# Mixture-of-experts stage of a fused two-block kernel: tokens and results as rounded parts

## The reference, cut to what matters

```python
h = modulate(rmsnorm(x, norm2_g), shift, scale)      # 256 tokens x 1024
probs = softmax(h @ router_w)                        # 16 experts in 4 groups of 4
# best group of each token, then its two best experts; combine = their normalised weights
for e in range(16):
    he = (silu(h @ w_gate[e]) * (h @ w_up[e])) @ w_down[e]   # 1024 -> 512 -> 1024
    out = out + combine[:, e:e + 1] * he
return rmsnorm(x + gate * out, final_norm_g)
```

## Time and profile before

| | us |
|---|---|
| median of 3 runs (lowest, highest) | 1445.51 (1444.1, 1450.73) |
| the profiled execution | 1446.31 |
| its span in the profile | 1444.9 |
| TensorE busy | 1341.1 (93%) |
| VectorE busy | 1044.2 (72%) |
| ScalarE busy | 711.7 (49%) |

### The profile page before, as it was taken

One profiled execution on the slowest core, in us unless ns is written; L12 is line 12 of the kernel. 1 busy time (PEld: TensorE's weight loads), 2 busy tenths in 40 slices (PEclk: granted clock), 3 DMA queues, 4 the chain that ended last, 5 costly groups with the idle time before them and its releaser, 6 DMA issues.

```text
span 1444.9 us, 20106 instructions
## 1 busy us (share of the span) xinstructions
PE 1341.1 (93%) x7872; PEld 1182.8 (82%) x7872; DVE 1044.2 (72%) x1502; ACT 711.7 (49%) x955; POOL 0.4 (0%) x5
## 2 busy tenths in 40 slices
PE   6979799999999997899997899999699999999996
PEld 6778699999777785899996688998687888887884
DVE  5676677786787787777876747866456869687685
ACT  3432455553575656454443643433146757566563
POOL 0000000000000000000000000000000000000000
PEclk9969899999999998999998999999699999999999
DMA  8729786865587775767563442220065978878772
GB/s 329 265 81 342 210 327 242 306 248 208 204 284 256 267 261 184 264 211 259 198 216 101 130 157 94 94 88 12 28 219 174 377 248 304 280 252 331 238 268 105
DMA packets 84349, 312.89 MB, mean 217 GB/s; under 512 B 9504, under 2 KB 9728, under 8 KB 83520
## 3 DMA queue, kind: packets, MB, share of 16 engines
q1 hardware_dynamic: 82080, 298.88, 58.6%
q10 hardware_dynamic: 2176, 12.74, 2.7%
HBM read 310.54 MB, written 1.05 MB: 216 GB/s over the span
## 4 chain that ended last, share of the span: by engine, by line
PE 82%; DVE 10%; ACT 3%; DMA 3%; issue 2%; SPq 0%; DVEq 0%; ACTq 0%
PE ps L445 81%; DVE w_low L404 2%; DMA ring<-stream 2%; DVE junk L404 1%; ACT w_high L404 1%; DVE rs L404 1%; DVE t_one L404 1%; PE ps L1042 1%; DMA ring<-moe 1%; DVE y_experts L404 1%; DVE sc L404 0%; DVE sm L404 0%; DVE rout L404 0%; ACT L404 0%; DVE t_two L404 0%
## 5 line engine op out<-in xcount | busy, mean ns | idle before, releaser
L404 DVE TENSOR_TENSOR w_low<-ring,w_high 128x1024 fp32r<-128x1024 f32 x368 | 442.0, 1222 | 166.7 <-ACT w_high L404 162.3
L404 ACT ACTIVATE w_high<-ring 128x1024 fp32r<-128x1024 f32 x368 | 385.6, 1058 | 294.1 <-PE ps L445 202.3
L445 PE MATMUL ps<-x_high,w_high 128*128 128x256 f32 (+1 forms) x784 | 235.5, 300 | 27.3 <-DVE x_low L404 21.1
L445 PE MATMUL ps<-x_low,w_high 128*128 128x256 f32 (+1 forms) x784 | 232.9, 297 | 0.0
L445 PE MATMUL ps<-x_high,w_low 128*128 128x256 f32 (+1 forms) x784 | 232.7, 297 | 0.0
L404 DVE CUSTOM_DVE_ANT_0 junk<-ring,cond 128x1024 f32<-128x1024 f32 x137 | 167.1, 1222 | 33.7 <-DMA ring<-stream 25.3
L445 PEld LDWEIGHTS ps<-x_high,w_high 128*128 128x128 f32 x784 | 154.5, 197 | 36.3 <-issue 12.9
L445 PEld LDWEIGHTS ps<-x_high,w_low 128*128 128x128 f32 x784 | 154.3, 197 | 2.8
L445 PEld LDWEIGHTS ps<-x_low,w_high 128*128 128x128 f32 x784 | 154.5, 197 | 2.5
L445 PE MATMUL ps<-h_high,w_high 128*128 128x256 f32 x512 | 145.4, 284 | 1.7 <-DVE h_low L404 1.0
L445 PE MATMUL ps<-h_low,w_high 128*128 128x256 f32 x512 | 144.9, 283 | 0.0
(11 more groups left out here) (302 smaller groups left out, 1999.1 us busy)
## 6 DMA issues: line engine op xcount, KB each, us to landing
ring<-stream SPq DMA_DIRECT2D x376, 512.0 KB, 4.7
ring<-moe SPq DMA_DIRECT2D x192, 512.0 KB, 4.8
tab_two<-tab ACTq DMA_DIRECT2D x1, 2824.0 KB, 14.4
gw<-gw ACTq DMA_DIRECT2D x1, 2304.0 KB, 15.5
cond<-cvec ACTq DMA_DIRECT2D x2, 512.0 KB, 5.3
x<-xT ACTq DMA_DIRECT2D x1, 1024.0 KB, 11.6
ctx_first<-ctxT ACTq DMA_DIRECT2D x1, 1024.0 KB, 5.6
ctx<-ctxT ACTq DMA_DIRECT2D x1, 1024.0 KB, 5.0
```

Source lines behind the costliest of these rows:

```text
L404: return op(*a, **k).then_inc(self.sem, 1)
L445: return pe.matmul(out, stationary, moving, start=start, stop=stop, skip_group_check=True)
```

## The change

- **Entry.** The norm, its gain and the modulation scale become one VectorE operation for each k-tile (into `t_one`); ScalarE adds the shift, writes `t_two` and signals each pair of tiles by `x_high`; the logits start per pair, k outermost.
- **Tokens as parts.** `pe.transpose` becomes a float32 product with the identity, which leaves the PSUM banks open (no stop). ScalarE writes the high part of the tokens, TensorE subtracts it from the bank by a product with the negative identity, ScalarE writes the rest as the low part. `onehot` and `scat` become float32r. The gather makes high and low parts in banks of their own: ScalarE copies one, VectorE the other, neither waiting for the other.
- **Order.** The gather's low copies go between VectorE's two picks of an expert; `diag`'s product moves into gate(0) after its first piece, the combine weights after gate(0).
- **Results as parts.** ScalarE writes high parts of results, VectorE the low parts; `scatter` makes two products for one of float32. `result_lows` and `summed` are new calls in the loop.
- **End.** The final norm is one pass.

```diff
-        self.XT = view("x_tokens", aB + 5120, 2048).rearrange("p (b d) -> p b d", b=2)
-        self.ONEHOT = view("onehot", ...)
-        self.SCAT = view("scat", ...)
+        self.XT = tuple(rounded("x_tokens_" + n, a, 2048)... for n, a in (("high", aB + 5120), ("low", aT1)))
+        self.ONEHOT = rounded("onehot", ...)
+        self.SCAT = rounded("scat", ...)
+        self.YES = tuple(rounded("y_experts_" + n, a, 2048)... for n, a in (("high", aT2), ("low", aB + 5120)))
+        self.YS = tuple(rounded("y_single_" + n, a, 1024) for n, a in (("high", aT1 + 1024), ("low", aT1)))
...
TensorE
-    pe.wait_ge(s.t2, 4 * MOD_MOE + 4)
-    for b in range(2):
-        for k in range(KT):
+    for k in range(KT):
+        if k % 2 == 0:
+            pe.wait_ge(s.x_high, x_splits(MOD_MOE) + k // 2 + 1)
+        for b in range(2):
             ins = mm(PS[:, 4 + b, 0:NE], m.T2[:, k, b * P:(b + 1) * P], m.par("rw", k * NE, NE), k == 0, k == KT - 1)
-            ins = pe.transpose(PS[...], m.T2[:, k, b * P:(b + 1) * P], m.ident)
+            ins = mm(PS[...], m.T2[:, k, b * P:(b + 1) * P], m.ident, k % 4 == 0, False)
...
+    for b in range(2):
+        pe.wait_ge(s.xt, b + 1)
+        for c in range(2):
+            ins = mm(PS[:, 2 * b + c, :], m.NEG, m.XT[0][:, b, c * 512:(c + 1) * 512], False, True)
+        ins.then_inc(s.xt_mm, 1)
+    pe.wait_ge(s.xt, 4)
     pe.wait_ge(s.onehot, 2)
+    for r in range(4):
+        if r == 3:
+            pe.wait_ge(s.xg_high, 1)
+            pe.wait_ge(s.xg_low, 1)
+        for part in range(2):
+            for j in range(2):
+                ins = tokens(PS[:, XG_BANKS[r][part], j * 256:(j + 1) * 256], part, 2 * r + j, slice(0, 256))
+            ins.then_inc(s.xg_mm, 1)
...
     def other_tokens():
+        pe.wait_ge(s.scat, 5)
+        pe.wait_ge(s.cw, 1)
         for k in range(KT):
-            pe.wait_ge(s.xg_low, 4 if k < 4 else k + 1)
-            for b in range(2):
-                ins = mm(PS[:, 4 + k % 4, ...], m.XT[:, b, ...], m.ONEHOT[:, b, 256:CAP], b == 0, b == 1)
-            ins.then_inc(s.xg_mm, 1)
+            pe.wait_ge(s.xg_high, 4 + max(k - 1, 0))
+            tokens(PS[:, 4 + k % 2, 0:CAP - 256], 0, k, slice(256, CAP)).then_inc(s.xg_mm, 1)
+            pe.wait_ge(s.xg_low, 4 + max(k - 1, 0))
+            tokens(PS[:, 6 + k % 2, 0:CAP - 256], 1, k, slice(256, CAP)).then_inc(s.xg_mm, 1)
...
     def scatter(i, r):
+        pe.wait_ge(s.y_add, Y_LOW[i] - (i > 0 and r < 2))
...
             if i == 0:
-                mm(out, m.YE[:, 0, blk], m.SCAT[:, 0, :], True, False)
-                ins = mm(out, m.YE[:, 1, blk], m.SCAT[:, 1, :], False, True)
+                for n in range(4):
+                    ins = mm(out, m.YES[n % 2][:, n // 2, blk], m.SCAT[:, n // 2, :], n == 0, n == 3)
             else:
-                ins = mm(out, m.YS[:, blk], m.SCAT[:, i + 1, :], True, True)
+                for n in range(2):
+                    ins = mm(out, m.YS[n][:, blk], m.SCAT[:, i + 1, :], n == 0, n == 1)
ScalarE
+    for k in range(KT):
+        if k % 2 == 0:
+            act.wait_ge(s.t2, 4 * MOD_MOE + k // 2 + 1)
+        A(m.T2[:, k, :], m.T1[:, k, :], ACT.Identity, s.x_high if k % 2 else None, bias=m.MOD[:, 120 + k:121 + k], apart=True)
+    A(m.NEG, m.ident, ACT.Copy, None, scale=-1.0)
...
+    def summed(p):
+        if EXPERTS[p] == (0, 3):
+            act.wait_ge(s.y_add, Y_SUMS[p])
+            for a in range(2):
+                A(m.YES[0][:, a, :], m.YE[:, a, :], ACT.Copy, s.y_out, apart=True)
...
     for p in range(NE):
         w = MOE_AT[p, "d", 0] - 4
         high_upto(w + 5)
+        if p > 0:
+            summed(p - 1)
         turned(p)
VectorE
-    rms_rows(9, m.X[:, :, :], m.T1[:, :, :])
-    modulate_norm(MOD_MOE, m.T1, "n2g", 120, 128)
+    sc2 = m.combo[:, 0:8]     # gain * (1 + scale), two small operations
+    root(9)
+    for k in range(KT):
+        op(vv.scalar_tensor_tensor, m.T1[:, k, :], m.X[:, k, :], sc2[:, k:k + 1], m.RSTD, ALU.mult, ALU.mult, inc=s.t2 if k % 2 else None, apart=k > 0)
...
+    def first_low(r):
+        vv.wait_ge(s.xg_mm, 2 * r + 2)
+        op(vv.tensor_copy, m.XGL[:, 2 * r:2 * r + 2, 0:256], PS[:, XG_BANKS[r][1], :]..., inc=s.xg_low, apart=True)
+        low_upto(W_MOE + r + 1)
...
+    def result_lows(p):
+        i, j = EXPERTS[p]
+        if j == 3:
+            for c in range(2):
+                vv.wait_ge(s.y_out, {1: 4, 2: 6, 0: 8, 3: 10}[i] - 1 + c)
+                # i == 0: YES[1][:, c] = YE[:, c] - YES[0][:, c]; else a half of YS[1] = PS - YS[0]
...
     low_upto(W_MOE + 12)
+    for k in range(KT):
+        vv.wait_ge(s.xg_mm, 8 + 2 * k + 2)
+        op(vv.tensor_copy, m.XGL[:, k, 256:CAP], PS[:, 6 + k % 2, 0:CAP - 256], inc=s.xg_low, apart=True)
     products(0)
     for p in range(NE):
         if p > 0:
+            if EXPERTS[p - 1][0] > 0:
+                result_lows(p - 1)
             low_upto(w + 3)
             products(p)
+            if EXPERTS[p - 1][0] == 0:
+                result_lows(p - 1)
...
+    result_lows(NE - 1)
     for r in range(4):
         results(3, r)
-    rms_rows(10, m.X[:, :, :], m.T1[:, :, :])
+    root(10)
     for k in range(KT):
-        op(vv.tensor_scalar, m.X[:, k, :], m.T1[:, k, :], m.par("fing", k), None, ALU.mult, inc=s.final, apart=k > 0)
+        op(vv.scalar_tensor_tensor, m.X[:, k, :], m.X[:, k, :], m.par("fing", k), m.RSTD, ALU.mult, ALU.mult, inc=s.final, apart=k > 0)
```

More of the change, by code:

```diff
@@ L329, in __init__ @@
         self.YE = view("y_experts", aKF, 2048).rearrange("p (a d) -> p a d", a=2)
-        self.YS = view("y_single", aT1 + 1024, 1024)
+        self.YES = tuple(rounded("y_experts_" + n, a, 2048).rearrange("p (a d) -> p a d", a=2) for n, a in (("high", aT2), ("low", aB + 5120)))
+        self.YS = tuple(rounded("y_single_" + n, a, 1024) for n, a in (("high", aT1 + 1024), ("low", aT1)))
     def place(self, n):
@@ L988, in tensor_program, with tokens @@
[L988 to L993, removed]
+    def tokens(out, part, k, slots):
+        for b in range(2):
+            ins = mm(out, m.XT[part][:, b, k * P:(k + 1) * P], m.ONEHOT[:, b, slots], b == 0, b == 1)
+        return ins
+    for b in range(2):
+        pe.wait_ge(s.xt, b + 1)
+        for c in range(2):
+            ins = mm(PS[:, 2 * b + c, :], m.NEG, m.XT[0][:, b, c * 512:(c + 1) * 512], False, True)
+        ins.then_inc(s.xt_mm, 1)
@@ L1461, in scalar_program @@
         act.wait_ge(s.xt_mm, b + 1)
-        A(m.XT[:, b, :], PS[:, 2 * b:2 * b + 2, :].rearrange("p c n -> p (c n)"), ACT.Copy, s.xt, apart=True)
+        A(m.XT[0][:, b, :], PS[:, 2 * b:2 * b + 2, :].rearrange("p c n -> p (c n)"), ACT.Copy, s.xt)
+    for b in range(2):
+        act.wait_ge(s.xt_mm, 3 + b)
+        A(m.XT[1][:, b, :], PS[:, 2 * b:2 * b + 2, :].rearrange("p c n -> p (c n)"), ACT.Copy, s.xt)
     for r in range(4):
-        act.wait_ge(s.xg_mm, r + 1)
-        A(m.XGH[:, 2 * r:2 * r + 2, 0:256], PS[:, 4 + r, :].rearrange("p (k s) -> p k s", k=2), ACT.Copy, s.xg_high, apart=True)
+        act.wait_ge(s.xg_mm, 2 * r + 1)
+        A(m.XGH[:, 2 * r:2 * r + 2, 0:256], PS[:, XG_BANKS[r][0], :].rearrange("p (k s) -> p k s", k=2), ACT.Copy, s.xg_high, apart=True)
         high_upto(W_MOE + r + 1)
@@ L1497, in scalar_program @@
     for k in range(KT):
-        act.wait_ge(s.xg_mm, 4 + k + 1)
-        A(m.XGH[:, k, 256:CAP], PS[:, 4 + k % 4, 0:CAP - 256], ACT.Copy, s.xg_high, apart=True)
+        act.wait_ge(s.xg_mm, 8 + 2 * k + 1)
+        A(m.XGH[:, k, 256:CAP], PS[:, 4 + k % 2, 0:CAP - 256], ACT.Copy, s.xg_high, apart=True)
     for p in range(NE):
@@ L2211, in sums @@
                 op(vv.tensor_tensor, half, half, PS[:, 1 + 2 * c, :], ALU.add, inc=s.y_add if c else None, apart=True)
+    def result_lows(p):
+        i, j = EXPERTS[p]
+        if j == 3:
+            for c in range(2):
+                vv.wait_ge(s.y_out, {1: 4, 2: 6, 0: 8, 3: 10}[i] - 1 + c)
+                if i == 0:
+                    op(vv.tensor_tensor, m.YES[1][:, c, :], m.YE[:, c, :], m.YES[0][:, c, :].bitcast(F32), ALU.subtract, inc=s.y_add, apart=True)
+                else:
+                    half = slice(c * 512, (c + 1) * 512)
+                    op(vv.tensor_tensor, m.YS[1][:, half], PS[:, 4 + c, :], m.YS[0][:, half].bitcast(F32), ALU.subtract, inc=s.y_add, apart=True)
     def results(i, r):
```

70 lines of the change are left out of this document (36 added, 34 removed).

## The result

The kernel after takes **1434.89 us** (median of five runs, 1433.92 to 1435.24), the kernel before in the same comparison 1445.73 us (five runs, 1444.1 to 1450.76). The ratio is 0.991, 95% interval 0.9892 to 0.9928. The profiled execution took 1434.94 us, its span is 1433.6 us.

A forecast was written before the change was run, and what follows sets the result against it. TensorE bounds from 1057 us, one serial path before. Gains 6.0 + 3.6 + 6.85 - 0.5 - 4.6 - 2.0 + 1.8 = 11.2 us off 1446.3 give 1435.1, as a median 1434.4 us; range 1428 to 1440.5 (8 in 10).

The forecast's parts named there:

- Entry: From the norm to the second gather: logits 3.6 us earlier, gate(0) at 1048.9 instead of 1057.01; gain 6.0 us.
- a clock that rises during the gather: First gather: 6.3 us from its start to gate(0), taken from a span of 5.0 to 7.4.
- transposes as the last wait before the counts: Entry: transposes end at 1037.9, after the routing at 1035.3, so the counts wait for them.
- full clock from the end of the transposes on: Rival for the entry: gain 9.1 us instead of 6.0, total 1431.3 us; chance 0.12.
- half clock behind the combine weights: In gate(0) and up(0): half clock after the tiny products, 3.5 us long at a cost of 1.7, counted for half.
- Second gather: 32 single products of 384 columns in 5.5 us plus a stall, for 10.4 before; gain 3.6 us (2.5 to 4.8).
- stall: Second gather: product k = 2 waits for VectorE's first low copy, behind the low part of piece 11; 1.1 us.
- Scatters: Scatters 1, 2 and 0: 64 single products for 64 float32 records, gain 6.85 us, less 0.5 for VectorE.
- The wait in gate(14): TensorE waits before scatter(0, 0) for the low parts of the sums, behind ScalarE's copies and VectorE's subtractions; loss 4.6 us.
- Half clock behind it: After TensorE's idling in gate(14) its clock falls; loss 2.0 us (1.6 to 2.3, zero if it holds).
- End: Scatter 3 and final norm: sums of squares start at once, 0.6 us, one-pass norm 1.2; together 1.8 us (1.2 to 2.2).
- VectorE or the ring becomes the bound: Rival in the expert stage: the scatters' 6.85 us are saved in vain, total gain 4.4, 1441.2 us; chance 0.12.

The follow-up runs named there:

- transpose mode: Changed kernel with `pe.transpose` back for the tokens' 16 transposes (their low parts then not the right ones): 1431.8 us, ratio 0.9888 to the kernel before.
- gather all: Changed kernel with all eight k-tiles of the second gather and `products(0)` made before the parts of weight piece 11: 1437.2 us, ratio 0.9923 to before.
- entry alone: Kernel before with only the new entry up to the logits (one-pass norm, ScalarE's shift, logits per pair), tokens and results in float32: 1438.9 us, 0.9936.
- late halves: Changed kernel with group 0 scattered in gate(15) and its sums' two halves taken apart, weight pieces between them: 1427.44 us, ratio 0.9852 to before.
- summed early: Changed kernel with ScalarE's copies of group 0's sums one weight piece earlier, scatter left in gate(14): 1435.86 us, ratio 0.9932 to before.
- results float32: Changed kernel with results unsplit in float32 again, `summed` and `result_lows` gone, all else as changed: 1434.29 us, ratio 0.9925 to before.
- doubled lows: Changed kernel with VectorE's two low-part subtractions of each single group's results done twice: 1440.45 us, ratio 0.9964 to before.
- late scatter: Changed kernel with group 0 scattered in gate(15) instead of gate(14): 1434.12 us, ratio 0.9912 to before.
- gather first: Changed kernel with the second gather's first two k-tiles made before the parts of weight piece 11: 1435.04 us, ratio 0.9913 to before.
- late scatter with gather first: Changed kernel with group 0 scattered in gate(15) and the second gather's first two k-tiles before piece 11: 1432.97 us, ratio 0.9887 to before.
- late halves with gather all: Changed kernel with both the edits of late halves and of gather all: 1431.78 us, ratio 0.9876 to before.

## Why the prediction was right, and where it wasn't

**The total is right by more than its steps deserve.** 1434.4 us forecast, 1434.89 measured. Four terms are off, by +2.0, -0.6, +1.1 and together -2.4 us, and that they cancel is luck.

- **Entry: the step that failed is "a clock that rises during the gather".** Start of the logits 1023.85 forecast, 1023.80 measured; transposes as the last wait before the counts, right; counts to gather 3.3 forecast, 3.4 measured. But the clock was up before the counts, and the gather took 4.4 us instead of 6.3. The rival "full clock from the end of the transposes on", which had 0.12 and 9.1 us, is what happened, with 8.0. I had the mechanism for it in hand and gave the row of the logits and transposes, which never lifted the clock, more weight than it has for other records. Transpose mode back (0.55 in the gather) shows it. In numbers: the gather started 0.8 us before its forecast, gave 1.9 us more, and from gate(0) to the second gather the kernel took 26.24 us for 25.5, since the half clock behind the combine weights, which I counted for half, came whole. (The prediction's own figures give 6.1, not 6.0.)
- **Second gather: right in size of the product (5.57 us without waits for 5.5), stall mis-sized.** 1.1 us forecast; gather all shows 7.02 - 5.57 = 1.45. The old gather, 10.4 us in the sum, is 10.02 from its start to gate(1), and 10.4 - 5.5 - 1.1 is 3.8, not 3.6.
- **Scatters: right where they can be seen.** From turn(5) to turn(7) 1.08 us is gained (1.7 - 0.5 forecast), from turn(10) to turn(12) 1.66 (1.7 forecast). Another 0.9 us from turn(9) to turn(10) is none of theirs, nor of the change: there the profile of before waits 0.58 us for `w_low` and 0.26 for `he`, and takes 18.16 us, while entry alone, with the same code there, doesn't wait and takes 16.85. Most of the +1.1 is the luck of one execution.
- **The wait in gate(14): 4.6 us forecast, 4.55 measured, by the chain that was foretold.** Half clock behind it: 3.4 us at 0.52 are 1.6 lost, 2.0 forecast; in transpose mode some 6.0 us at half clock followed the same wait, 3.0 lost, so this size is not a fixed one. Late halves, summed early and the float32 results each take away their part of it.
- **Down(15): not in the sum.** The earlier trace rows have nothing on it; the 1.50 us wait for `he_low` is in both kernels, and half clock followed it in after's profile (0.50 in the last window above), not in before's. 1.5 us.
- **End: 1.8 forecast, 0.9 measured.** The final norm gives 1.23 us (1.2 forecast). Its other part, 0.6 us by sums that start at once, came to 0.06, and the sums themselves took 4.26 us against 3.62 in the earlier trace rows: two steps of scatter 3 and most of the sums ran at half clock after a wait of 0.58 us. In summed early, where the clock held in scatter 3, that part came to 0.56 us.
- **The rival "VectorE or the ring becomes the bound" had its share where I priced nothing.** After's waits don't show it, but doubled lows does: 3.9 us more on VectorE cost 8.9, some 1.4 of them perhaps luck. That less work for TensorE before turn(10) would be mostly lost, gather all can't show (above).

## What to carry to other kernels

When an operand of TensorE has to be made by other engines, place the making by the piece, not by the result: two subtractions in one lump cost 2.4 us of waiting and in one of two executions the clock behind it, the same two with weight pieces between them 0.36 and 0.37. A wait of the bounding engine has two prices, its length and the half clock behind it. The second isn't fixed: nothing behind 2.42 us in one execution, 1.6 us behind 4.55 in another, 1.5 behind 1.50 in a third. And read a stage from its own first record: the stages of the two best versions differed by under 0.1 us where their medians differed by 4.3. But take more than one profile of a code before believing a difference of 1 or 2 us between two of them.

## What the runs showed of the hardware that I had not expected

**The same wait, two clocks.** In down(15) every one of the 13 kernels profiled waits 1.50 or 1.51 us for `he_low`. In eight of them (after, late scatter, doubled lows, results float32, entry alone, gather first, late scatter with gather first, gather all) 3 to 4 us at 0.50 follow, without a stretch of 3.5 us of idling as in the earlier trace rows; in five (before, summed early, transpose mode, late halves, late halves with gather all) the clock holds. The windows of summed early at that place:

```profile
1404.60:1408.00 3.40, 3.40 (x17) 2.68 (x16) 2.74 (x3) 1.11 (x2) 0.00 (x0) 1.00 0.00 0
```

It ran 17 records in 3.40 us, after 8 in 3.20 us. The same happens once more in scatter 3, behind waits of 1.41 and 0.58 us: after falls there, summed early doesn't. Together that is 2.65 us between turn(15) and the end (26.97 and 24.32 us), in kernels whose instructions there are the same. What decides it no run here shows.

**Behind small products the clock fell without an idle TensorE.** The combine weights' 20 products of 4 columns run from 1057.70 us after, in the midst of gate(0)'s and up(0)'s work. Behind them the clock fell, as two more windows of after show:

```profile
1060.00:1062.00 2.00, 2.00 (x7) 1.54 (x8) 1.10 (x2) 1.41 (x3) 0.00 (x0) 0.65 0.68 229
1062.00:1064.00 2.00, 2.00 (x6) 1.63 (x5) 0.00 (x0) 0.00 (x0) 0.00 (x0) 0.50 0.56 205
```

In nine more of the profiled kernels it fell in the same place, in before and entry alone right behind the same 20 products, and in transpose mode alone, where they come 1.1 us later, it stayed at 1.00. The logits' 32 products of 16 columns, dense for 7 us, left it at 0.50; it rose during the 32 products with the identity behind them (the window from 1036.00 us has 0.71).
